# Two more buffers for modulation chunks, and three of eight residual adds behind each norm moved to GpSimd

## The reference, cut to what matters

```python
shift1, scale1, gate1, shift2, scale2, gate2 = mod      # silu(c) @ w_mod + b_mod, in six parts
h = rmsnorm(x, g_mix_pre) * (1 + scale1) + shift1
y, ctx_state = mixer(h)
x = x + gate1 * rmsnorm(y, g_mix_post)
h = rmsnorm(x, g_ffn_pre) * (1 + scale2) + shift2
x = x + gate2 * rmsnorm(conv_ffn(h, w_ffn_in, w_ffn_conv, w_ffn_out), g_ffn_post)
```

## Time and profile before

| | before |
|---|---|
| median of 3 runs | 1746.85 us (1740.14 to 1747.06) |
| the profiled execution | 1745.92 us, its span 1744.1 us |
| TensorE / Vector / ScalarE / GpSimd busy | 93% / 63% / 41% / 7% |
| mean granted TensorE clock | 0.965 of full speed |

### The profile page before, as it was taken

How to read it: one execution, slowest core, us unless ns; L and a number is a source line. 1 busy time by engine, 2 the same in 40 slices (tenths; PEclk the granted TensorE clock), 3 DMA queues, 4 the chain that set the end, 5 groups by cost and what they waited for, 6 DMA issues and landing times.

```text
span 1744.1 us, 32070 instructions
## 1 busy us (share of the span) xinstructions
PE 1615.8 (93%) x11897; PEld 1547.1 (89%) x11897; DVE 1102.9 (63%) x2066; ACT 716.7 (41%) x1189; POOL 113.8 (7%) x121
## 2 busy tenths in 40 slices
PE   7798998959999999999879979989799999999995
PEld 4797887959999999999879967779699999999995
DVE  4796666767777767778863238863666642466624
ACT  5632664235443124442252127653566531343410
POOL 1331110000000000000000032500000000000000
PEclk9898999979999999999999979999899999999998
DMA  9233002513334533335412220102022231222211
GB/s 343 87 127 112 2 2 70 175 46 97 108 109 141 195 132 109 108 125 190 168 67 72 73 64 2 44 1 85 13 73 72 72 100 57 72 72 74 89 67 61
DMA packets 43774, 160.35 MB, mean 92 GB/s; under 512 B 5184, under 2 KB 6208, under 8 KB 43440
## 3 DMA queue, kind: packets, MB, share of 16 engines
q1 hardware_dynamic: 40896, 152.00, 26.4%
q0 software_dynamic: 1584, 6.38, 1.1%
q10 hardware_dynamic: 1216, 0.92, 0.2%
HBM read 155.74 MB, written 3.54 MB: 91 GB/s over the span
## 4 chain that ended last, share of the span: by engine, by line
PE 79%; DVE 6%; issue 4%; ACT 2%; DMA 1%; DVEq 1%; ACTq 0%; SPq 0%
PE ps L1458 29%; PE ps L1459 29%; PE ps L1636 4%; PE ps L1665 3%; PE ps L1493 3%; PE ps L1651 3%; DVE x L951 1%; DMA ring<-in_wmodt 1%; PE ps L1472 1%; PE ps L1471 1%; PE ps L1585 1%; PE ps L1586 1%; DVE ring L838 1%; DVE wlo L830 1%; ACT work L579 1%
## 5 line engine op out<-in xcount | busy, mean ns | idle before, releaser
L513 ACT ACTIVATE whi<-raw 128x1024 fp32r<-128x1024 f32 (+1 forms) x166 | 185.6, 1120 | 576.2 <-PE ps L1459 494.1
L1458 PE MATMUL ps<-hh,whi 128*128 128x320 f32 x928 | 289.3, 312 | 12.3 <-DVE wlo L830 12.2
L1459 PE MATMUL ps<-hl,whi 128*128 128x320 f32 x928 | 288.0, 310 | 0.0
L1459 PE MATMUL ps<-hh,whi 128*128 128x320 f32 x928 | 288.0, 310 | 0.0
L1458 PE MATMUL ps<-hl,whi 128*128 128x320 f32 x928 | 287.9, 310 | 0.0
L1459 PE MATMUL ps<-hh,wlo 128*128 128x320 f32 x928 | 287.9, 310 | 0.0
L1458 PE MATMUL ps<-hh,wlo 128*128 128x320 f32 x928 | 287.9, 310 | 0.0
L830 DVE TENSOR_TENSOR wlo<-raw,whi 128x1024 fp32r<-128x1024 f32 (+1 forms) x166 | 218.3, 1317 | 74.9 <-ACT whi L513 74.5
L1458 PEld LDWEIGHTS ps<-hh,whi 128*128 128x128 f32 x928 | 175.3, 189 | 13.8 <-DVE wlo L830 13.8
L1459 PEld LDWEIGHTS ps<-hh,whi 128*128 128x128 f32 x928 | 175.5, 189 | 0.0
L1458 PEld LDWEIGHTS ps<-hl,whi 128*128 128x128 f32 x928 | 175.3, 189 | 0.0
(11 more groups left out here) (217 smaller groups left out, 3179.8 us busy)
## 6 DMA issues: line engine op xcount, KB each, us to landing
raw<-in_w SPq DMA_DIRECT2D x134, 512.0 KB, 3.5
work<-in_wmodt SPq DMA_DIRECT2D x54, 512.0 KB, 3.6
raw<-in_w SPq DMA_DIRECT2D x32, 704.0 KB, 4.1
ring<-in_wmodt SPq DMA_DIRECT2D x26, 512.0 KB, 3.7
work<-in_wmod SPq DMA_DIRECT2D x16, 512.0 KB, 6.1
work<-in_rpb POOLq DMA_DIRECT2D x8, 448.0 KB, 4.5
x<-in_x SPq DMA_DIRECT2D x8, 320.0 KB, 6.7
out_x<-x SPq DMA_DIRECT2D x8, 320.0 KB, 2.2
```

The lines of the kernel that those rows point to most:

```text
L513: nc.scalar.activation(whi[:, s, 0:kk * P], raw[:, s, 0:kk * P], ACT.Copy).then_inc(s_hi, 1)
L1458: T.matmul(bankA[s], slot(w, s, k), h[:, k, 0:HT], start=st, stop=sp_)
L1459: last = T.matmul(bankB[s], slot(w, s, k), h[:, k, HT:NT], start=st, stop=sp_)
```

## The change

It has two parts. First, `ring0` gets two more buffers, laid at the start of `region_f` over q and k of the attention. Chunks 12 and 13 are issued into them when attention's output is done and its k and v are stored; from there on the pairs alternate between buffers 2, 3 and 0, 1, so each pair is issued one turn sooner. The counts of the loading semaphores and the indices of the later phases are written anew to match; those phases do what they did.

Second, in the norms n = 1, 3, 5, 7 GpSimd adds chunks 1, 3 and 5 into x. Since its instruction is a plain add over all 640 columns, Vector writes the gated product y * coef * inverse_rows of these chunks into a buffer (`gated_home`), in two instructions of 512 and 128 columns, in place of the scale. Vector waits for GpSimd's add of chunk k + 1 before its own add of chunk k + 2. Chunks 0, 2, 4, 6 and 7 stay with Vector. The loop over chunk pairs becomes straight code.

```diff
@@ -205,6 +205,7 @@
         v0 = over("v0", [P, 6, 2 * P])
         cwide0 = over("cwide0", [P, 2, 1024])
         ring0 = [over(f"ring0_{b}", [P, 1024])[:, :] for b in range(2)]
+        ring0 += [at(f"ring0_{b + 2}", [P, 1024], F32, region_f + 4096 * b)[:, :] for b in range(2)]
         assert pos[0] <= region_f + 2 * FH * NT * 4
         cwide1 = at("cwide1", [P, 2, 1024], F32, region_c)
         product1 = at("product1", [P, 1024], F32, region_c + 8192)[:, :]
@@ -217,6 +218,7 @@
         tn = ring(1280, 2, NT)
         hf = ring(2560, 2, NT)
         acc = tn[0]
+        gated_home = {1: tn[1], 3: hf[1], 5: tn[1]}
 
         ub = ring(0, 2, UW)
         cb = ring(2 * UW, 2, CW)
@@ -269,7 +271,8 @@
         s_csilu = sem("c_activated")
         s_cwide = sem("wide_c_loaded")
         s_cwsilu = sem("wide_c_activated")
-        s_mch = [sem("mod_chunk_loaded_0"), sem("mod_chunk_loaded_1")]
+        s_mch = [sem("mod_chunk_loaded_0"), sem("mod_chunk_loaded_1"), sem("mod_chunk_loaded_2"),
+                 sem("mod_chunk_loaded_3")]
         s_mused = sem("mod_chunk_summed")
         s_again = sem("tables_loaded_again")
         s_mraw = [sem(f"mod_weights_loaded_{i}") for i in range(4)]
@@ -430,16 +433,23 @@
                 wide(14 + s, s, w8, 14 + s, 8)
             sp.wait_ge(s_oe, 30)
             sp.dma_start(cwide1[:, :, :].rearrange("p a n -> p (a n)"), a["cwide"]).then_inc(s_cwide, 16)
+            sp.wait_ge(s_out, 32)
+            for b in range(2):
+                chunk_in(12 + b, 2 + b, ring0)
             sp.wait_ge(s_mused, 12)
             for b in range(2):
-                chunk_in(12 + b, b, ring0)
-            with sp.Fori(0, 3) as p:
+                chunk_in(14 + b, b, ring0)
+            with sp.Fori(0, 2) as p:
                 for s in range(2):
                     wide(2 * p + (16 + s), s, w8, 2 * p + (16 + s), 8)
                     sp.wait_ge(s_mused, 4 * p + (2 * s + 14))
                     for b in range(2):
-                        chunk_in(4 * p + (2 * s + 14 + b), b, ring0)
-            for n in (22, 23, 24):
+                        chunk_in(4 * p + (2 * s + 16 + b), 2 - 2 * s + b, ring0)
+            wide(20, 0, w8, 20, 8)
+            sp.wait_ge(s_mused, 22)
+            for b in range(2):
+                chunk_in(24 + b, 2 + b, ring0)
+            for n in (21, 22, 23, 24):
                 wide(n, n % 2, w8, n, 8)
             sp.wait_ge(s_t, 24)
             chunk_in(26, 1, ring1)
@@ -952,7 +962,25 @@
                             out=xs, in0=tn[s][:, f:t], scalar=coef[:, layer, st, which, bass.ds(k, 1)],
                             in1=xs, op0=ALU.mult, op1=ALU.add)
                     last.then_inc(s_tu, 1)
-                rows_then(n, y, add)
+
+                def gated(k, home):
+                    dve.wait_ge(s_tu, 8 * n + k)
+                    for st, f, t in SEG:
+                        last = V.scalar_tensor_tensor(
+                            out=home[:, f:t], in0=part(y, k, f, t - f), scalar=coef[:, layer, st, which, k:k + 1],
+                            in1=inverse_rows[:, f:t], op0=ALU.mult, op1=ALU.mult)
+                    last.then_inc(s_t, 1)
+
+                for k in (0, 2, 4):
+                    scale_row(n, y, k, 0)
+                    gated(k + 1, gated_home[k + 1])
+                    dve.wait_ge(s_tu, 8 * n + k + 2)
+                    add(k, 0)
+                for k in (6, 7):
+                    scale_row(n, y, k, k - 6)
+                dve.wait_ge(s_tu, 8 * n + 8)
+                for k in (6, 7):
+                    add(k, k - 6)
 
             dve.wait_ge(s_cst, 1)
             V.tensor_tensor(cst[:, :, 2:4], csilu[:, :].rearrange("p (k s) -> p k s", s=2), cst[:, :, 0:2].bitcast(F32),
@@ -1180,7 +1208,7 @@
 
                 def after(h, s):
                     if not (isinstance(h, int) and 2 * h + s == n - 1):
-                        mods(2 * h, s)
+                        mods(h, s)
 
                 def add_square(k, s):
 
@@ -1229,17 +1257,18 @@
                         V.tensor_tensor(chunk(ffl, h), fft, chunk(ffh, h).bitcast(F32), ALU.subtract).then_inc(s_ffl, 1)
                 run((layer, f"fin{half}"), f, after if mods is not None else None)
 
-            def mods_mix(i, s):
+            def mods_mix(h, s):
                 for b in range(2):
-                    mod_chunk(2 * i + (2 * s + 12 + b), b, i + (s + (5, 9)[b]), ring0, cwide0, product0)
+                    home, n = (2 + b, 1) if s == 0 else (b, (4, 8)[b] + (s + 1) // 2)
+                    mod_chunk(4 * h + (2 * s + 12 + b), home, h + n, ring0, cwide0, product0)
 
             def mods_fin(m0, n0):
                 return lambda h: mod_chunk(h + m0, 1, h + n0, ring1, cwide1, product1)
 
             def mods_fout(m0, n0, n1):
-                def f(i, s):
+                def f(h, s):
                     for b in range(2):
-                        mod_chunk(2 * i + (2 * s + m0 + 2 + b), b, i + (s + 1 + (n0, n1)[b]), ring1, cwide1, product1)
+                        mod_chunk(4 * h + (2 * s + m0 + 2 + b), b, 2 * h + (s + 1 + (n0, n1)[b]), ring1, cwide1, product1)
                 return f
 
             def ffn(layer):
@@ -1251,10 +1280,10 @@
                 dve.wait_ge(s_out, 32 * (layer + 1))
                 if layer == 0:
                     dve.wait_ge(s_cwsilu, 2)
-                    ffn_half(0, 0, mods_fin(26, 16))
-                    y_phase((0, "fout0"), False, mods_fout(37, 12, 27))
-                    ffn_half(0, 1, mods_fin(53, 35))
-                    y_phase((0, "fout1"), True, mods_fout(64, 20, 46))
+                    ffn_half(0, 0, mods_fin(26, 12))
+                    y_phase((0, "fout0"), False, mods_fout(37, 8, 23))
+                    ffn_half(0, 1, mods_fin(53, 31))
+                    y_phase((0, "fout1"), True, mods_fout(64, 16, 42))
                     finish_mod(80, 40, 96, 6, ((0, 3), (1, 0), (1, 1), (1, 2), (1, 3)))
                     dve.wait_ge(s_coef, 16)
                 else:
@@ -1403,9 +1432,18 @@
                     stage("B", it, i, JOBS * (2 * it + i - 1) if it else 0)
             pool.wait_ge(s_stage, 24)
 
+            def post_norm(n):
+                for k in (1, 3, 5):
+                    pool.wait_ge(s_t, 8 * n + k + 1)
+                    pool.wait_ge(s_tu, 8 * n + k + 2)
+                    G.tensor_tensor(chunk(x, k), chunk(x, k), gated_home[k], ALU.add).then_inc(s_tu, 1)
+
+            post_norm(1)
+
             pool.wait_ge(s_unit, UNITS[(1, "in")][0] + 2)
             pool.dma_start(qk[:, 8:13, CTX0:PR0], a["kctx1"]).then_inc(s_ctx1, 16)
             pool.dma_start(v1[:, 4, :], a["vctx1"]).then_inc(s_ctx1, 16)
+            post_norm(3)
             pool.wait_ge(s_hl, 24 + 2)
 
             def load_bias(e, head):
@@ -1438,6 +1476,8 @@
                 pool.wait_ge(s_stage, staged[0])
                 for half in range(2):
                     mask_bias(2 * i + half, 2)
+            for n in (5, 7):
+                post_norm(n)
 
 
         @block.tensor
```

## The result

| | before | after |
|---|---|---|
| median | 1743.85 us (1740.14 to 1747.06, 4 runs) | 1725.14 us (1723.46 to 1728.0, 4 runs) |
| profiled execution, span | 1745.92, 1744.1 us | 1724.94, 1723.2 us |
| ratio, 95% interval | | 0.9895 [0.9866, 0.9924] |

The kernel became 1.05% faster, by 18.7 us in the medians and 20.9 in the two spans. (The median of before shown ahead of the prediction was of three runs; one more was made with those of the changed kernel.) The forecast was 1728 us for the median and 1727.3 for the profiled execution. The page of after: busy times, and the chain that ended last by engine. Lines of the program are numbered anew; the square sum is L1549, the scale L927, the add L961, the gated pair L969, GpSimd's add L1439.

The account below looks back on a forecast made before the run. The prediction took TensorE, busy 93% of the span, to bound the kernel except where it stands still. 1745.92 - 10.2 (buffers) - 8.4 (norms) = 1727.3 us for the profiled execution, 1728 for the median; range 1721 to 1737.

Parts of the forecast that it names:

- Ring's loads: Layer 0's mixing stage: Vector's stall of 2.58 us a turn on chunk loads goes to nothing with two more buffers.
- TensorE as the bound: Layer 0's mixing stage: TensorE's 8.18 us a turn bounds once Vector needs 6.44; last square sum starts 7.8 us earlier.
- the six stalls of 2.5 us: Layer 0's mixing stage: the saving is not the stalls' sum, since TensorE bounds; buffers bring 10.2 us together.
- The clock: Last square sum to norm 1's first scale: 3.29 us in place of 5.66 with TensorE at 2.4 GHz, another 2.4 us.
- Vector's part: Norms 1, 3, 5, 7: wait, scale and gated pair beside GpSimd take 0.16 + 0.735 + 0.965 = 1.86 us.
- GpSimd's leg: Norms 1, 3, 5, 7: handover, 640-column add and Vector's wait take 0.23 + 1.25 + 0.16 = 1.64 us.
- 8.54 + 3X: Total of one norm in us for a GpSimd add of X over 1.47; with 2.02 it is 14.60.
- the spare time of 0.22 us: Norms' turns: GpSimd's leg of 1.64 us is covered by Vector's 1.86 with this to spare, but not the third time.
- Norms: Norms 1, 3, 5, 7: 12.73 us against 14.84 from first scale to last add, 2.1 us each, 8.4 in all.
- loads stay late: Rival, mixing stage: ring's loads late through shared DMA engines or SP held up; only norms count, 1737.5 us; chance 0.07.
- the slower outcome: Rival, norms: GpSimd adds of 2.95 us pay back the buffers' 10.2; at 3.7, 0.5% slower, about 1755 us; chance 0.03.
- Rival (b): Norms: GpSimd's add takes 1.6 to 2.1 us, from start-up or sharing; total 1731 to 1737 us; chance 0.17.

Follow-up runs that it names:

- the filler in the kernel before: Kernel before, plus 27 matmuls of constants into an unused PSUM bank ahead of the last square sum of layer 0's mixing stage; one execution, 1742.82 us.
- the shorter add: Changed kernel with GpSimd adding 512 columns only, context columns of chunks 1, 3, 5 left out; first scale to last add 12.39 us.
- a filler: Changed kernel with own buffer for gated chunks 1 and 5, plus 12 constant matmuls ahead of the square sums of norms 1, 3, 5; 1721.09 us, ratio 0.9870.

## Why the prediction was right, point by point

**Ring's loads.** The stall went to nothing, with SP's queue in the order worked out. DMA was busy 0.74 and 0.66 of the turns from 304.17 and 312.33, where 0.56 was estimated: in these first turns Vector runs ahead of TensorE and draws its chunks faster. In the next two it was 0.59 and 0.54. It did no harm. **TensorE as the bound.** 8.16 us a turn against 8.18; last square sum 7.90 us earlier against 7.8; one unit's end to the last sum 2.61 against 2.62, taken from layer 1. That the six stalls of 2.5 us are not worth 15 was the main point, and the run with the buffers alone bears it out. **The clock.** 2.25 us against 2.4, and shown to be the clock by the filler in the kernel before. **Vector's part.** The gated pair takes 0.92 us a turn against 0.965, the same 0.92 as with both operands in SBUF and GpSimd idle: PSUM costs it nothing.

**GpSimd's leg was mis-sized, and other terms cancel it.** Its add takes 1.55 us and not 1.25, the handovers 0.17 + 0.10 and not 0.23 + 0.16: the leg is 1.82 us against 1.64 in the first turn, and 1.80 in the last, since its first handover is 0.14 us there. It counts once a norm, in the last turn, +0.16 us. Vector's part of a turn is 1.76 us and not 1.86 (its wait 0.11, not 0.16), 0.09 less in each of two turns, and the stretch up to the end of add 0 is 0.04 shorter. So 12.67 lies this near to 12.73 in part by luck.

By the prediction's own formula, 8.54 + 3X from X = 1.47 on, an add of 1.55 us would have given 13.19 us, 0.5 more a norm. It did not, since the handovers and Vector's wait were priced too high. But the spare time of 0.22 us in the turns isn't there: GpSimd's add ends at 355.34, and Vector goes on at 355.38. The turns are only just covered; the shorter add showed that Vector still bounds them.

The rows chosen for the width were the two quickest by the column, 128x671 at 1.31 us and 128x896 at 1.75, both 1.95 ns a column. The same 128x671 took 1.95 us in its other instance, and other rows with two full operands had the right pace:

```profile
L1386 POOL TENSOR_TENSOR work<-work 128x669 f32<-128x669 f32 x1 | 1.6, 1627 | 0.1
L1329 POOL TENSOR_TENSOR kl<-qk,kh 128x768 fp32r<-128x768 f32 x4 | 7.3, 1819 | 0.3
```

That is 2.43 and 2.37 ns a column, and 1.547 / 640 is 2.42. The two measured widths say more: 1.547 - 1.273 = 0.274 us for 128 columns is 2.14 ns a column, which leaves 0.18 us that do not go by width; as an estimate from these two, 768 columns take 1.82 us, as the row has it. Why the two chosen rows were quicker is not shown. L1417 repeats an operand over 8 columns; but L1384 and L1386 both read two shifted views of one tile, so that alone isn't it. Nor was the upper bound of 2.02 the worst row: L1390, 64x669, took 2.17 us.

The estimate from the Trainium skill, "GPSIMD Engine Reference", section "Elementwise — side-by-side cycle accounting", 1.41 us, was nearer than mine, and still 0.14 short; its advice to keep elementwise work on Vector did not decide here, where GpSimd idles and the leg is covered.

**Norms.** 12.67 us against 12.73 from first scale to last add, 2.17 us a norm against 2.1. Norm 1 gave 1.43 only: TensorE, at 1.2 GHz, was late with the square sums. The prediction took it for granted that those follow the adds; with faster adds they became the bound. In that execution the granted clock was 0.51 from 353.8 to 360.7 us. In the second execution of the same kernel it was 0.51 from 354.4 to 357.9 us only, and norm 1 took 17.23 us like the others; and with the norms alone it was norm 3 that had 0.50 from 858.7 to 865.5, and took 17.83. So this 0.6 to 0.75 us belongs to how long TensorE stays at 1.2 GHz, and not to norm 1. What sets that was not tried.

**Ruled out.** That loads stay late (no such wait is left), that GpSimd is slowed by sharing (1.535 against 1.547), and the slower outcome, which needed an add of 2.95 us or more. Rival (b) began at an add of 1.6 us, and the add took 1.55: it was a near miss in the add, though not in the total.

**Luck, and not explained.** The profiled execution came out at 1724.94 us, 2.4 under the forecast: the changed stretches gave 0.5 less than forecast, and 2.8 us came from unchanged work. Of these, the 1.54 us in layer 0's FFN are the fall of the clock described above, which before's profile had, the changed kernel's first one had not and its second one had: chance of the executions. The 1.81 us before the mixing stage stay open. Over the runs with unchanged work there, the first square sum came between 294.61 and 297.75 us, and before's profile is the latest of them; the stretch from norm 4's first scale to norm 5's took 342.0 to 346.5 us.

## What to carry to other kernels

A stall in a stage is worth what the next bound leaves of it: six stalls of 2.5 us were worth 7.9 us, because TensorE needed 8.16 us of the 9.02, plus 2.3 us for a clock that no longer fell ahead of the last sum. Work can be handed to an idle, slower engine if its leg is covered turn by turn, and more cheaply if the instructions beside it read one operand from PSUM; price its instruction by rows with two full operands and of more than one width, and look where the handover has no cover. When a chain on Vector is shortened, look at what only followed it, here TensorE's small sums at 1.2 GHz. And profile both kernels twice: two profiles of the changed kernel differ by 1.56 us in a stretch of 480 us that nobody touched.

## What was not expected of the hardware

A pair of Vector instructions of 512 and 128 columns took 0.92 us with one operand in PSUM beside a GpSimd add, and 1.58 us with both in SBUF; GpSimd's add took 1.55 us in both. The loss fell on Vector alone, and was 0.66 us where waiting for the add's end would give 0.85 (it began 0.70 us into the 1.55). The Trainium skill, "SBUF — State Buffer", section "Who interferes with whom", says that a Vector instruction with two SBUF inputs contends with a GpSimd instruction that reads SBUF, and one with at most one does not; both halves agree with these runs.

TensorE began the square sums of norm 1 at 1.2 GHz after 3.82 us without work; it began the last sum of the mixing stage at 2.4 GHz after 1.34 us, and norm 1's sums after 1.14 us behind a filler. In norm 3 of the same execution it began after 3.83 us at 2.4 GHz and fell 0.3 us later (granted 0.50 from 852.2 to 855.6 us). Whether the clock then fell again behind a later idle stretch of about 2.5 us differed between executions of one kernel.
